# Attention stage: branch projections in pairs by seven half products, branch a before branch b, five weight slots

## The reference, cut to what matters

```
ga, gb, gc = (jax.nn.sigmoid(t) for t in pr[11:14])     # pr = h @ w_in, 1024 columns each
y = ga * (o_a @ w_proj_a) + gb * (o_b @ w_proj_b) + gc * (o_c @ w_proj_c)
return y @ w_out
```

## Time and profile before

| what | value |
|---|---|
| three timed runs | 2806.43, 2803.72, 2806.21 us; median 2806.21 us |
| profiled execution, its own time | 2803.49 us |
| its span | 2801.4 us, mean granted TensorE clock 0.986 |
| PE busy | 2685.6 us (96%) |
| DVE busy | 1288.8 us (46%) |
| ACT busy | 520.7 us (19%) |
| attention stage | 752.4 us to 1154.8 us of the span |

### The profile page before, as it was taken

The page is one execution under the profiler, slowest core; times in us unless marked ns, Lnnn a source line. Parts: engine busy times, 40 slices in busy tenths (PEclk is TensorE's granted clock), DMA queues, the critical chain, the costliest instruction groups (busy, mean ns, idle before and its releaser), DMA issues.

```text
span 2801.4 us, 32571 instructions
## 1 busy us (share of the span) xinstructions
PE 2685.6 (96%) x12874; PEld 1833.9 (65%) x12874; DVE 1288.8 (46%) x2382; ACT 520.7 (19%) x854; POOL 171.5 (6%) x140
## 2 busy tenths in 40 slices
PE   6999999999899999999799999989999999999997
PEld 3688888887555555785343333334495877888886
DVE  4255666654446456545311111155473335654644
ACT  3122121222233233211100000031322113000001
POOL 1122211220000000241000000000000000000000
PEclk9999999999999999999899999999999999999998
DMA  9622111211121121236599999932103421323330
GB/s 352 209 61 57 55 52 45 60 30 38 31 61 53 38 65 48 81 85 226 228 409 409 409 409 409 409 113 74 32 1 84 134 68 46 89 79 88 91 90 30
DMA packets 327676, 374.62 MB, mean 134 GB/s; under 512 B 10033, under 2 KB 273030, under 8 KB 324230
## 3 DMA queue, kind: packets, MB, share of 16 engines
q1 hardware_dynamic: 327286, 371.93, 38.9%
q10 hardware_dynamic: 272, 1.05, 0.1%
HBM read 370.85 MB, written 2.10 MB: 133 GB/s over the span
## 4 chain that ended last, share of the span: by engine, by line
PE 91%; DVE 4%; DVEq 1%; DMA 1%; ACT 1%; issue 1%; SPq 0%; ACTq 0%
PE psum L1747 31%; PE psum L2049 12%; PE psum L2205 6%; PE psum L1476 4%; PE psum L1424 4%; PE psum L720 3%; PE psum L1120 2%; PE psum L1934 2%; PE psum L815 2%; PE psum L728 2%; PE psum L2739 2%; PE psum L1975 2%; PE psum L705 2%; PE psum L1310 2%; PE psum L1362 2%; PE psum L1339 2%
## 5 line engine op out<-in xcount | busy, mean ns | idle before, releaser
L1747 PE MATMUL psum<-arena 128*128 128x256 f32 x4144 | 907.2, 378 | 1.7 <-DVEq L1770 1.2
L1747 PEld LDWEIGHTS psum<-arena 128*128 128x128 f32 x4144 | 778.9, 189 | 116.4 <-issue 4.7
L2049 PE MATMUL psum<-arena 128*64 128x512 f32 x1536 | 347.6, 597 | 3.0 <-issue 2.1
L2049 PEld LDWEIGHTS psum<-arena 128*64 128x64 f32 x1536 | 104.8, 136 | 217.5 <-issue 214.5
L1779 DVE TENSOR_TENSOR arena<-psum,arena 128x256 f32<-128x256 f32 x66 | 28.0, 425 | 312.6 <-ACT arena L1792 191.5
L2205 PE MATMUL psum<-arena 128*128 128x512 f32 (+1 forms) x448 | 170.5, 538 | 0.0
L1980 DVE SCALAR_TENSOR_TENSOR arena<-psum,arena 128x512 f32<-128x512 f32 x64 | 48.0, 750 | 246.4 <-PE psum L1975 245.8
L2205 PEld LDWEIGHTS psum<-arena 128*128 128x128 f32 x448 | 85.9, 192 | 82.3 <-issue 78.8
L1476 PE MATMUL psum<-arena 128*128 128x512 f32 x256 | 116.2, 595 | 0.0
L1754 POOL TENSOR_TENSOR arena<-arena 128x512 f32<-128x512 f32 x34 | 48.4, 1425 | 1103.6 <-DMA arena<-in_w_in 639.1
L1424 PE MATMUL psum<-arena 128*128 128x256 f32 x448 | 103.6, 382 | 0.0
(11 more groups left out here) (386 smaller groups left out, 3367.6 us busy)
## 6 DMA issues: line engine op xcount, KB each, us to landing
arena<-in_w_gate SPq DMA_DIRECT2D x64, 1024.0 KB, 18.4
arena<-in_w_up SPq DMA_DIRECT2D x64, 1024.0 KB, 16.2
arena<-in_w_down SPq DMA_DIRECT2D x64, 1024.0 KB, 18.0
arena<-in_w_in SPq DMA_DIRECT2D x120, 512.0 KB, 4.2
arena<-in_ada_w SPq DMA_DIRECT2D x24, 1024.0 KB, 7.2
arena<-in_w_up SPq DMA_DIRECT2D x32, 512.0 KB, 5.1
arena<-in_w_down SPq DMA_DIRECT2D x32, 512.0 KB, 4.8
arena<-in_w_out SPq DMA_DIRECT2D x16, 512.0 KB, 4.0
```

The lines of the kernel that those rows point to most:

```text
L1747: mm = pe.matmul(psum[:, base + b, c * HALF:(c + 1) * HALF], w, v, start=(first and q == 0 and m in (0, 2, 3, 4)), stop=(last and q == KC ...
L2049: mm = pe.matmul(psum[64 * e:64 * e + 64, bank + n, :], tokens(e, 2 * q + k), w[:, k, 512 * n:512 * n + 512], start=(q == 0 and k == 0), s ...
```

## The change

The branch projection becomes a second pair job of the same seven-product form. There are now 16 such jobs `p`; p = 2q is the gate of query `q` (fillers of t = 0 and 1), p = 2q + 1 its branch projection (t = 2 and 3). Queries 0 to 3 serve branch a, all eight chunks; queries 4 to 7 serve branch b. DVE forms sums of weights for each of the 16 jobs and runs all four recombination phases for each. The products need sums of the tokens of `aT` and `bT` too: `dve_branch_sums` forms them on DVE at the end of t = 0 and t = 1 of q = 0 (branch a) and q = 4 (branch b), one in place in columns that no product reads any more. The multiplication by the gate (and for branch b the addition) is done for both chunks at once, `dve_gated`, at the end of t = 0 of the next query. The whole projection of the next query stands in t = 0. The weights have a fifth slot (3), except that the last four units go to slots 4 to 7; `dve_item_done` multiplies in place, which frees a tile.

```diff
-        ws.phase("attn", 1, [(sources[n],) + unit_place(4 + n % 4) for n in range(len(sources))],
-                 [4 + n % 4 for n in range(len(sources))])
+        def attn_place(n):
+            if n >= unit_of_fill(PAIRS_Q - 1, 0):
+                return 4 + n - unit_of_fill(PAIRS_Q - 1, 0)
+            return (3, 4, 5, 6, 7)[n % 5] if n > Q0 else (4, 5, 6, 7, 3)[n]
+        ws.phase("attn", 1, [(sources[n],) + unit_place(attn_place(n)) for n in range(len(sources))],
+                 [attn_place(n) for n in range(len(sources))])
...
+        def form_fill_sums(eng, p):
+            for u in fill_units(p):
+                ws.arrived(eng, "attn", 0, u)
+            if p == 0:
+                eng.wait_ge(sem("head_out"), HEADS + 1)
+                eng.wait_ge(sem("swapped"), KEYS)
+            elif p == 8:
+                eng.wait_ge(sem("scores_1"), 16)
+            if p:
+                eng.wait_ge(sem("fill_phase"), 3 * p)
+            weight_sums(eng, *fill_weights(p), fill_sums(p), "fill_sums")
+
+        def halves(x):
+            return x.rearrange("p (j e) (h n) -> p e h j n", e=2, h=2)
+
+        def dve_branch_sums(dve, b, part):
+            x = halves((aT, bT)[b])
+            t1, t2, t3 = branch_t[b]
+            if part == 0:
+                if b == 0:
+                    dve.wait_ge(sem("values_in"), 3)
+                dve.tensor_tensor(t1, x[:, 1, 1], x[:, 0, 1], ALU.subtract)
+                dve.drain()
+                dve.tensor_tensor(x[:, 0, 1], x[:, 0, 1], x[:, 0, 0], ALU.subtract)
+                dve.drain()
             else:
-                done(eng, "attn", 0, unit_of_fill(q - 1, 1))
-            weight_sums(eng, *gate_weights(q), gate_sums(q), "gate_sums")
+                dve.tensor_tensor(t2, x[:, 1, 1], x[:, 0, 1], ALU.subtract)
+                dve.drain()
+                dve.tensor_tensor(t3, x[:, 1, 0], t2, ALU.subtract)
+                dve.drain()
+                dve.sem_inc(sem("branch_sums"), 1)
...
+        def pe_fill(pe, p, phase):
...
+            if phase >= 2:
+                pe.wait_ge(sem("fill_parts"), 4 * p + phase - 1)
...
-        def pe_branch(pe, q, e, part):
-
-            u = unit_of_fill(q, 2 + e)
-            x = (aT, bT)[q % 2]
-            if part == 0:
-                ws.arrived(pe, "attn", 0, u)
-                pe.wait_ge(sem("gate_parts"), 4 * q + 3 + e)
-            for k in range(4 * part, 4 * part + 4):
-                mm = pe.matmul(psum[:, 6 + e, :], ws.dst("attn", u)[:, k, :], x[:, k, :], start=(k == 0), stop=(k == KC - 1))
...
+        def dve_gated(dve, q):
+            o, c = fill_result(2 * q + 1), 2 * (q % 4)
+            y = yT[:, c:c + 2, :].rearrange("p e n -> p (e n)")
             dve.wait_ge(sem("gate_out"), 2 * q + 2)
+            dve.tensor_tensor(o, o, m_gate, ALU.mult)
+            dve.drain()
+            if q >= 4:
+                dve.tensor_tensor(y, y, o, ALU.add)
                 dve.drain()
             dve.sem_inc(sem("branch_out"), 1)
 
         def pe_filler(pe, s, part):
             q, r = s // 4, s % 4
-            if r < 2:
-                pe_gate(pe, q, 2 * r + part)
-            else:
-                pe_branch(pe, q, r - 2, part)
+            pe_fill(pe, 2 * q + r // 2, 2 * (r % 2) + part)
...
-                if t < 2 and q < PAIRS_Q - 1:
-                    pe_item_proj(pe, n, t)
+                if t == 0 and q < PAIRS_Q - 1:
+                    pe_item_proj(pe, n, None)
...
-                if t == 0 and q:
-                    dve_branch(dve, q - 1, 1)
-                if t == 1:
-                    dve_gate(dve, q, 1)
-                if t == 2:
-                    dve_gate(dve, q, 3)
+                p = 2 * q + t // 2
+                if t % 2:
+                    dve_fill(dve, p, 1)
+                elif p:
+                    dve_fill(dve, p - 1, 3)
                 dve_max(dve, s, 0)
                 dve_max(dve, s, 1)
                 dve_scale(dve, s, 0)
...
                 turned_copy(dve, s, 1)
-                if t == 0:
-                    dve_gate(dve, q, 0)
-                if t == 1:
-                    dve_gate(dve, q, 2)
-                if t == 3:
-                    dve_branch(dve, q, 0)
-                    if q < PAIRS_Q - 1:
-                        form_gate_sums(dve, q + 1)
+                if t == 0 and q:
+                    dve_gated(dve, q - 1)
+                if t % 2 == 0:
+                    dve_fill(dve, p, 0)
+                else:
+                    dve_fill(dve, p, 2)
+                    if p < 2 * PAIRS_Q - 1:
+                        form_fill_sums(dve, p + 1)
+                if q % 4 == 0 and t < 2:
+                    dve_branch_sums(dve, q // 4, t)
...
-                if n < 2:
-                    done(pool, "attn", 0, unit_of_fill(PAIRS_Q - 2, 3))
+                if n == 0:
+                    done(pool, "attn", 0, unit_of_fill(3, 3))
+                elif n == 1:
+                    pool.wait_ge(sem("branch_out"), PAIRS_Q)
```

More of the change, by code:

```diff
@@ L1082, in mixed_block_kernel @@
         m_gate = at.take(2 * S)
-        late = [at.take(S) for _ in range(3)]
+        late = [at.take(S) for _ in range(2)]
         a_prob = [at.take(T) for _ in range(2)]
@@ L1086, in mixed_block_kernel @@
         a_stat = at.take(2, 4)
+        gate_a, gate_u = at.take(HALF), at.take(HALF)
+        branch_sum = Carve(arena, CT_LO - 4096 + 1536, CT_LO).take(2 * S)
+        branch_t = [(HT[:, 0:4, 0:C], HT[:, 4:8, 0:C], last[:, 6:8, :].rearrange("p k (h n) -> p (k h) n", h=2))
+                    for last in (cT, aT)]
         SCALE = 64 ** -0.5
@@ L1368, in act_values, with fill_units, fill_weights, fill_sums @@
             act.activation(cT[:, q, :], psum[:, values_place(q), :], ACT.Copy).then_inc(sem("attended"), 1)
[L1370 to L1377, removed]
+        def fill_units(p):
+            return unit_of_fill(p // 2, 2 * (p % 2)), unit_of_fill(p // 2, 2 * (p % 2) + 1)
+        def fill_weights(p):
+            return [ws.dst("attn", u) for u in fill_units(p)]
+        def fill_sums(p):
+            if p < 8:
+                kept = [cT[:, 3 + m, :].rearrange("p (k n) -> p k n", n=P) for m in range(3)]
             else:
@@ L1380, in gate_sums @@
                 kept = [area.take(KC // 2, P) for _ in range(3)]
[L1381 to L1387, removed]
+            return kept + [fill_weights(p)[1].rearrange("p (k h) n -> p h k n", h=2)[:, 0]]
+        def form_fill_sums(eng, p):
+            for u in fill_units(p):
+                ws.arrived(eng, "attn", 0, u)
+            if p == 0:
@@ L1403, in pe_gate @@
+        PHASES = [(0, 1), (4,), (3, 5), (6, 2)]
+        def pe_fill(pe, p, phase):
+            wa, wb = fill_weights(p)
+            sums = fill_sums(p)
+            if p % 2:
+                b = p // 8
+                x, t1, t2, t3 = (aT, bT)[b], *branch_t[b]
+                t0 = halves(x)[:, 0, 1]
+            else:
+                x = HT[:, :, C:T]
+                t0, t1, t2, t3 = (ht_t[:, :, m, :] for m in range(4))
             if phase == 0:
-                for e in range(2):
-                    ws.arrived(pe, "attn", 0, u + e)
@@ L1406, in pe_gate @@
-                if q == 0:
+                for u in fill_units(p):
+                    ws.arrived(pe, "attn", 0, u)
+                if p == 0:
                     pe.wait_ge(sem("head_root"), HEADS)
                 else:
-                    pe.wait_ge(sem("branch_out"), 2 * q - 1)
+                    pe.wait_ge(sem("fill_parts"), 4 * p - 1)
             if phase == 1:
-                pe.wait_ge(sem("gate_sums"), q + 1)
-                if q == 0:
+                pe.wait_ge(sem("fill_sums"), p + 1)
@@ L1413, in pe_gate @@
+                if p == 0:
                     pe.wait_ge(sem("head_out"), HEADS + 1)
                 else:
-                    pe.wait_ge(sem("branch_out"), 2 * q)
+                    pe.wait_ge(sem("fill_parts"), 4 * p)
+                if p % 2:
+                    pe.wait_ge(sem("branch_sums"), p // 8 + 1)
             if phase >= 2:
-                pe.wait_ge(sem("gate_parts"), 4 * q + phase - 1)
+                pe.wait_ge(sem("fill_parts"), 4 * p + phase - 1)
             for at_, m in enumerate(PHASES[phase]):
```

85 lines of the change are left out of this document (38 added, 47 removed).

## The result

| | kernel before | changed kernel |
|---|---|---|
| median of six runs each | 2805.53 us (2803.72 to 2807.53) | 2816.31 us (2815.27 to 2818.55) |
| ratio, 95% interval | 1 | 1.004 (1.003 to 1.005) |
| profiled execution, span | 2803.49, 2801.4 us | 2817.28, 2815.5 us |
| attention stage, first scores to end of last filler | 402.3 us | 412.9 us |

The change made the kernel 10.8 us slower, 0.4%. The prediction said 2814.5 us; its sum of waits less gain was 9.8 us.

What follows compares the result with a forecast made beforehand. PE's work was taken to bound the attention stage: waits of 23.6 us less 0.5 already paid, net 23.1, less 13.3 gained, give +9.8 us. Forecast 2814.5 us, likeliest range 2809 to 2819, with rivals 2 and 1 2802 to 2821.

Steps and rivals of the forecast that it cites:

- What bounds the kernel, and the gain on PE: Attention stage: PE's work sets the time; half products save PE 1.66 us a query, 13.3 us for eight.
- t = 1, q = 1 to 3: PE waits for the second half's scaling, behind DVE's copy, gating and two recombination phases: 1.7 us for three.
- t = 1, q = 5 to 7: Branch b's longer gating delays recombination phase 0, whose PSUM bank PE wants, and the first maximum: 5.6 us in all.
- t = 2, q = 1, 2, 3, 5, 6: PE waits for the second scaling, behind DVE's copy, phase 2, weight sums and phase 3: 3.3 us for five.
- t = 2, q = 7: Last query, no item work as cover: PE waits for the scalings, with two restarts, 1.5 us.
- rival 4: Strided operations of the branch sums cost double: +19 us, 2823; chance 0.04.
- Rival 1: Waits are as reckoned and PE's clock falls after the three long ones: +14.9 us, 2818 to 2821; chance 0.09.
- The third wait: Last of the three longest PE waits, at t = 2 of q = 4, behind the branch sums, 2.5 to 2.6 us.
- Rivals 2 and 3: 2: branch sums don't hold PE, +0.4 us, chance 0.18; 3: PE never waits, 13.3 us gained, chance 0.12.
- rival 2: Branch sums don't hold PE, or DVE runs further ahead: waits 14 us, +0.4 us, 2804 to 2807; chance 0.18.
- What costs nothing: SP's first weight loads, POOL's second weight sums in the merge stage and ACT's eight more copies: no cost.

Runs made afterwards that it cites:

- first: Changed kernel without the four DVE operations forming the branch token sums: stage 402.15 us, kernel 2804.72 us, ratio 0.9993.
- third experiment: Changed kernel with gating and both branch-sum halves moved in DVE's list to t = 0, behind the scalings: stage 396.64 us, kernel 2798.35 us, ratio 0.9972.
- fourth: Changed kernel with gating, branch sums and also phase 3 of the recombination moved behind DVE's scalings: stage 391.46 us, kernel 2796.01 us, ratio 0.9959.
- sixth: Changed kernel with the next query's projection in two parts again, in t = 0 and t = 1: stage 405.77 us, kernel 2810.45 us, ratio 1.0017.

## Why the prediction was right

**What bounds the kernel, and the gain on PE.** Right. A query's own PE work went from 51.96 to 50.29 us, 1.67 less; the forecast said 1.66. Eight queries are 13.4 us.

**The waits, step by step** (us; measured is the step less its own length):

| place | forecast | measured |
|---|---|---|
| t = 1, q = 1 to 3 | 1.7 | 1.2 |
| t = 1, q = 5 to 7 | 5.6 | 5.1 |
| t = 2, q = 1, 2, 3, 5, 6 | 3.3 | 2.8 |
| t = 2, q = 7 | 1.5 | 2.1, of which 0.65 POOL |
| t = 1, q = 0 | 1.8 | 1.6 |
| t = 2, q = 0 | 3.25 | 4.9, of which 1.7 clock |
| t = 1, q = 4 | 3.2 | 4.7, of which 1.7 clock |
| t = 2, q = 4 | 3.25 | 2.0 |
| t = 0; t = 3 | 0 | 0; 0.3 in q = 7 |
| sum | 23.6 | 24.7 |

24.7 less 13.4 and less the 0.8 us that the last query waited before (some 0.26 in each of t = 1, 2 and 3; the forecast took 0.5) is 10.5; the stage grew by 10.6. The forecast was 9.8, and its places are the measured ones: where the first, third, fourth and sixth experiments take DVE's work away from a step or give PE more to do there, the waits of that step shrink or go. The small waits came out 0.1 to 0.2 us shorter each; at t = 1 that is DVE reaching its maximum in 3.39 us rather than 3.6. The branch sums were to cost 9.4 us and to decide the sign; they cost 10.8 with the clock.

**Where it was lucky.** The closeness of 9.8 to 10.6 is in part a cancellation. Without the clock the waits would have been about 22.5 us by the lengths above, 1.1 under the forecast; the clock, which the forecast put at nothing, added 2.2. The median that it named, 2814.5 us, lies between the profiled execution and the median of the first three runs, each plus 9.8 (2813.3 and 2816.0).

**The operation that the trace had not shown.** The strided branch sums took 1.23 us each, the contiguous row's value, so rival 4 fell.

**The rivals.** Rival 1 happened in part: the clock fell after two waits, not three, and one fall paid most of its cost back in the next step, so that by the steps' lengths all falls together cost about 1.7 + 1.7 - 1.2 = 2.2 us in place of 5. The third wait was no test of it: reckoned at 2.6 us, it came out at 1.30, DVE having caught up during the fall one step before. I had set its chance at 0.09, too low, in view of rows 7, where a gap of the same length was followed by a fall. The argument against it, full work on both sides of a wait, failed: so it was around the two waits that were followed by one. Rivals 2 and 3 fell with the sign. The argument against rival 2, that DVE's list is in order whatever its average load, is what the third experiment shows: with the same load the loss is a gain.

**What costs nothing.** The slots and ACT's copies cost nothing that shows: the stretch after the stage is the same to 0.2 us, and t = 0 and t = 3 of queries 0 to 6 have their own lengths. The merge stage did cost something, ahead of its start: its first sum of weights on POOL met DVE's scaling in the last query, 0.65 us, which the forecast had at nothing.

## What to carry to other kernels

When an engine in strict order sits in a latency chain (maximum, exponential, scaling) for a busy TensorE, count what stands in its list between the last result it handed over and the next link of the chain, not its share of busy time: here DVE was busy for two thirds, and yet the 10.4 us of branch sums at the wrong place cost 10.8 us. Put such work right behind the link that TensorE waits for, in the step where TensorE has the most of its own to do; first and last rounds, which lack part of that work, need their own count. Giving the work to GpSimd instead moved the wait: it slowed the very VectorE operation that TensorE was waiting for.

## What the runs showed of the hardware

- Idle times of TensorE in otherwise full work can be followed by a half-clock stretch. Inside the stage, over the changed kernel and the experiments, all eleven from 1.9 to 4.9 us were, and the four of 1.25 to 1.30 us were not. Ahead of the stage the same idle time was followed by a fall in some executions only: 2.48 us at one place in 10 of 12, 2.07 us some 15 us earlier in 2 of 12, 2.07 us right ahead of the first scores in none. Where full work followed, one fall cost about 1.7 us, less where the engine would have waited right after.
- Ahead of the stage, where TensorE waits for VectorE between the last head's levels, the kernel before and its variant with the moved projection have the same code, and their stages began at 752.4 and 758.3 us, with a mean granted clock ahead of it of 0.99 and 0.98. So single times of this kernel differ by several us without a cause in the change, and the clock goes with it; the length of a stage repeated to 0.02 us.
- The branch sums, subtractions over four rows of 256 columns that do not adjoin, took 1.23 us each on VectorE, as an operation on 1024 adjoining columns does.
- With GpSimd active in SBUF, a VectorE scaling of 128x768 took 1.69 us for 0.62, and ended 0.4 us after the GpSimd operation that it met.
